# A hybrid diffusion step: modulation rows as four column tiles of 128 in place of two of 256

## What is computed

```python
def modulation(cvec, w_mod, b_mod):              # w_mod: 1024 x 6144
    m = (jax.nn.silu(cvec) @ w_mod + b_mod)[..., None, :]
    return jnp.split(m, 6, axis=-1)              # sh1, sc1, gt1, sh2, sc2, gt2

def ada_norm(x, g, shift, scale):
    return rmsnorm(x, g) * (1.0 + scale) + shift

for l in range(DEPTH):                           # DEPTH = 2
    h = ada_norm(x, g_pre_mix[l], sh1, sc1)
    y = mixer(h, ...)
    x = x + gt1 * rmsnorm(y, g_post_mix[l])
    h = ada_norm(x, g_pre_ffn[l], sh2, sc2)
    y = hier_moe(h, ...)
    x = x + gt2 * rmsnorm(y, g_post_ffn[l])
```

## The kernel before

| blocks | place |
|---|---|
| 0, 1 | start of the neighbourhood attention, after the context scores and after the first unit's scores |
| 2, 3 | start of the latent attention, in the same two positions |
| 4 | inside the loop of the latent attention, at unit 16 |
| 5 | after the latent attention, before the gates and branches are merged |
| 6 to 11 | the tail, among transposes, router logits (L1300 copies them), counting and listing of the experts' tokens |

## Time and profile before

### The profile page before, as it was taken

How to read it: one execution, slowest core, us unless ns; L and a number is a source line. 1 busy time by engine, 2 the same in 40 slices (tenths; PEclk the granted TensorE clock), 3 DMA queues, 4 the chain that set the end, 5 groups by cost and what they waited for, 6 DMA issues and landing times.

```text
span 2179.6 us, 29979 instructions
## 1 busy us (share of the span) xinstructions
PE 1911.7 (88%) x12236; PEld 1532.5 (70%) x12236; DVE 780.6 (36%) x1418; ACT 564.7 (26%) x909; POOL 191.4 (9%) x200
## 2 busy tenths in 40 slices
PE   3799898999999796999818998989999997979992
PEld 1798555779999453878618975656899993548781
DVE  2422557652322135111062227477432222341113
ACT  1411251642211021111152104426331211201113
POOL 0102410000000000011050032100000000000104
PEclk8799999999999898999958999999999998989996
DMA  9313342211221408999682123121122214289995
GB/s 349 131 61 81 138 147 106 70 59 59 88 68 59 183 34 311 357 353 356 237 307 83 56 56 138 40 78 59 59 83 73 78 49 183 105 303 358 356 344 203
DMA packets 193262, 340.91 MB, mean 156 GB/s; under 512 B 9884, under 2 KB 113708, under 8 KB 192812
## 3 DMA queue, kind: packets, MB, share of 16 engines
q1 hardware_dynamic: 163644, 266.16, 35.4%
q10 hardware_dynamic: 21728, 44.83, 5.9%
q0 software_dynamic: 7776, 28.32, 3.7%
HBM read 309.50 MB, written 41.30 MB: 161 GB/s over the span
## 4 chain that ended last, share of the span: by engine, by line
PE 77%; DVE 10%; DMA 5%; issue 3%; ACT 3%; SPq 1%; POOL 1%; ACTq 0%; DVEq 0%; POOLq 0%
PE pair L1596 68%; PE opair L1596 5%; PE pair L1642 3%; DMA ring<-in_w_out 2%; DVE mid L1178 1%; DMA r<-mod_rows 1%; DMA ring<-in_w_up 1%; DVE r L1434 1%; ACT r L959 1%; SPq L533 1%; DVE mid L1190 1%; DMA ysT<-in_mod_aux 0%; DVE mid L1070 0%; DVE mid L1219 0%; DVE mid L1307 0%
## 5 line engine op out<-in xcount | busy, mean ns | idle before, releaser
L1596 PEld LDWEIGHTS pair<-r,ring 128*128 128x128 f32 x2176 | 252.5, 195 | 22.0 <-issue 19.4
L1596 PE MATMUL pair<-r,ring 128*128 128x128 f32 x2176 | 253.0, 278 | 6.0 <-DMA ring<-in_w_up 6.0
L1596 PE MATMUL pair<-ring,r 128*128 128x512 f32 x456 | 207.8, 611 | 34.1 <-DMA ring<-in_w_out 31.1
L1596 PE MATMUL pair<-hT_r,mid_r 128*128 128x320 f32 x768 | 237.3, 309 | 0.0
L1596 PE MATMUL pair<-r_r,ring_r 128*128 128x320 f32 x832 | 211.8, 309 | 2.2 <-DVE ring_r L1051 2.2
L1642 PE MATMUL pair<-cst,mid 128*128 128x128 f32 (+1 forms) x668 | 107.3, 300 | 112.2 <-DVE mid L1070 81.6
L1642 PEld LDWEIGHTS pair<-cst,mid 128*128 128x128 f32 (+1 forms) x668 | 81.9, 152 | 156.9 <-DVE mid L1070 85.8
L1596 PE MATMUL pair<-ysT_r,mid_r 128*128 128x256 f32 (+1 forms) x768 | 172.0, 315 | 16.3 <-issue 16.3
L1596 PEld LDWEIGHTS pair<-ring,r 128*128 128x128 f32 x456 | 86.7, 195 | 140.2 <-issue 132.2
L1596 PE MATMUL pair<-mid_r 128*128 128x320 f32 x576 | 178.9, 311 | 1.6 <-issue 1.6
L1596 PE MATMUL pair<-r_r,mid_r 128*128 128x256 f32 (+2 forms) x576 | 180.0, 313 | 0.0
(11 more groups left out here) (248 smaller groups left out, 2949.7 us busy)
## 6 DMA issues: line engine op xcount, KB each, us to landing
ring<-in_w_mod SPq DMA_DIRECT2D x27, 2048.0 KB, 9.6
ring<-in_w_gate SPq DMA_DIRECT2D x34, 1024.0 KB, 7.3
ring<-in_w_up SPq DMA_DIRECT2D x34, 1024.0 KB, 12.5
ring<-in_w_down SPq DMA_DIRECT2D x34, 1024.0 KB, 11.1
ring<-in_w_in SPq DMA_DIRECT2D x24, 1024.0 KB, 7.1
expert_out<-r ACTq DMA_DIRECT2D x34, 512.0 KB, 7.5
ring<-in_w_in SPq DMA_DIRECT2D x8, 2048.0 KB, 13.8
ring<-in_w_branch SPq DMA_DIRECT2D x12, 1024.0 KB, 5.1
```

What stands on the lines that cost most here:

```text
L1596: return nc.tensor.matmul(out, lhsT, rhs, start=first, stop=last, skip_group_check=True)
```

## The change

The two constants become 4 and 128: a block is four column tiles of 128 columns, with results at output partitions 0, 32, 64 and 96. All helpers take their loops from `MT` and their widths from `MW`.

```diff
 MOD = 6 * D
 NMOD = MOD // 512
-MT, MW = 2, 256
+MT, MW = 4, 128
 EPS = 1e-6
```

## The result

The changed kernel takes 2206.54 us, the median of 4 runs (2204.61 to 2209.29); the kernel before, run beside it, 2178.25 (4 runs, 2177.26 to 2179.66). The ratio is 1.0130, 95% interval 1.0115 to 1.0145: **+28.3 us**. Measured again later, with 4 and 15 runs, it was 2206.19 against 2179.61, ratio 1.0119 (1.0104 to 1.0135). The forecast was +13.9 us, with 2199 as the upper end. The direction was right, the size half.

The account below looks back on a forecast made before the run. TensorE held 77% of the chain of waits, but its saving counted only where waited for. Terms of +6.8 us a layer, 13.6 for two, plus prologue 0.3 gave +13.9 on 2177.66: 2191.6 us, range 2180 to 2199.

Parts of the forecast that it names:

- TensorE's block: Each modulation block on TensorE: four tiles side by side take 1.9 us, saving 1.7 us a block.
- that rival: Modulation blocks on TensorE: four tiles don't share the array, product stays at 3.6 us; +19.5 us, 2197; chance 0.13.
- VectorE: Reading and scaling each block's tiles: 8 operations instead of 4, 2.4 us, +0.67 us a block.
- The overlap rival: Block rows on VectorE: short operations overlap, rows stay 1.7 us; +2.8 us in all, 2180.5; chance 0.17.
- Prologue: Four blocks before the layers: stores issued 3.5 us later find free engines; +0.3 us, bounds 0 and +3.5.
- C: Block 4, inside the latent loop: VectorE's maximum waits for TensorE, so the shorter product counts; −1.7 us a layer.
- D: Block 5, before the merge: product hidden, VectorE's rows and the stores lengthen the chain; +1.3 us a layer.
- A: Start of the neighbourhood attention: VectorE waits for later loads, then works longer; +3.3 us a layer.
- B: Start of the latent attention: later loads and longer VectorE rows, the product's saving hidden; +1.4 us a layer.
- E: The tail: block 7 −1.1, VectorE's rows +1.34, SyncE's queue before the first expert's weights +2.3; +2.5 us a layer.
- the clock falls: TensorE at half clock in first units of both attentions; +4 us a layer, 2199.6; chance 0.12.

Follow-up runs that it names:

- b_dve: The kernel before with each VectorE operation of a modulation block cut in two column halves, 8 a block; 2181.69 us, +2.4.
- a_byrow: The changed kernel with one DMA per conditioning row instead of per tile, 2 loads and 2 stores a block; 2187.73 us, +9.5 against the kernel before.
- b_pe4: The kernel before with four TensorE tiles, rows kept in two-tile layout, 6 VectorE operations, 2 loads and 2 stores a block; 2179.95 us, ratio 1.0004.
- a_twice: The changed kernel with the layers' modulation products computed twice; 2207.28 us, +27.9 against the kernel before.
- b_sp_dve: The kernel before with SyncE's loads and stores and VectorE's operations doubled, TensorE's blocks left as they were; 2204.96 us, +25.6.
- the fill: 64 unread TensorE records added behind each of blocks 0, 1, 2, 3 and 5 of a layer; on the kernel before 2180.49 us, +2.1.
- a_fill: The changed kernel with 64 unread TensorE records added behind each of blocks 0, 1, 2, 3 and 5 of a layer; 2205.32 us, +27.0 against the kernel before.
- the tail's fill: The changed kernel with 64 unread TensorE records added behind blocks 6, 8 and 9 only; 2206.52 us, against 2206.19 without.
- b_pe4_twice: The four-tile kernel with two-tile rows (`b_pe4`) with every block's products computed twice; 2186.70 us, +8.4 against the kernel before.

## Why the prediction was half right

**TensorE's block: right.** 64 records in 1.93 us at full clock, forecast 1.9. The four tiles share the array; that rival is out.

**VectorE: right.** 2.4 us a block, forecast 2.4. The overlap rival named its own test, starts under 0.25 us apart; they are 0.29 to 0.31 apart. `b_dve` shows that the rival's mechanism exists (0.21), but only between operations on the same partitions. VectorE's part grew from 1.73 to 2.44 us a block while TensorE's shrank from 3.62 to 1.93. The Trainium skill, TensorEngine Tiling (Array Packing), Performance Considerations, says that packing speeds up TensorE but not the evacuation of PSUM, and that this should be vectorized over tiles. The trace agrees that it was not sped up. For the vectorizing no run stands alone: between `a_byrow` (8 operations, 2187.7) and `b_pe4` (6 operations and other stores, 2180.0) lie 7.8 us.

**Prologue: right.** The four stores are issued at 39.41 and the last has landed at 41.63, forecast 41; VectorE's first normalisation starts 0.88 us later, forecast 0.3. Kernels with the old prologue start it up to 1.0 later than the trace before, so this is not told from the forecast, nor from nothing.

**C and D: right.** C is 13.32 us for 15.01 between the two maxima named at `a_twice`, in both layers, so -1.7 (the table of the result, from another start, has -2.0); D is +1.25. The forecast was -1.7 and +1.3.

**A: too small.** Forecast +3.3, measured +3.86 by the chain above, in the second layer +3.9. I had counted the four loads as +1.7; they are +2.16, because the third does not follow the second at once (issues at 255.97, 256.84, 258.11 and 258.96).

**B and the first term of E: the step that failed, and by the cause that I had as a rival.** The forecast put TensorE's work behind the lengthened waits at no extra time. It runs at half clock.

For B the forecast was +1.4. Measured were about +3.2 and +3.4 (in the first layer later by 2.6 before it and by 5.8 behind it; in the second 16.3 and 19.7). The SyncE and VectorE terms came as forecast: the copy L1164 at B is 1.3 and 1.4 us later than the place's first L1155. Behind it the half clock adds 1.7, of which 0.3 is won back. The other 0.6 lies between A and B, where six transposes take 1.54 us for 0.87.

The rival "the clock falls" priced this at 4 us a layer for A and B together; I gave it 0.12 and put nothing of it into the sum, and it left the tail out. Its objection, that the stretches are short and covered by the waits, holds at A (`a_byrow`) and failed at B and in the tail. What the clock costs is shown on `b_sp_dve`: the fill alone takes 7.2 us back. Half right the rival was in its cause, too: I wrote "a 1.9 us block and a longer wait". `b_sp_dve`, with blocks of 3.6 us, shows that the wait suffices, and `b_pe4` that the shorter block does.

**E: the largest miss, +5.7 and +4.4 us for +2.5.** Along the chain of waits, first and second layer:

| term | forecast | measured |
|---|---|---|
| block 7, to the last logits' copy | -1.1 | +1.6, +1.3 |
| VectorE's rows, to block 9's first store (853.54 before, 861.93) | +1.34 | +1.4, +1.4 |
| SyncE's queue, to the first expert's weights (858.53 before, 869.16) | +2.3 | +2.2, +2.2 |
| their landing | 0 | +0.4, -0.7 |

VectorE's and SyncE's terms are right. The first is wrong by 2.7 and 2.4 us: the block is 1.56 us shorter, but the logits and transposes in front of it take 2.4 us more at half clock, a cost that the sum did not have; the rows behind it take the forecast's 0.7 more. In `a_byrow` TensorE's wait there is the same 3.80 us and the stretch up to the last logits comes out 1.8 us shorter in one layer and 0.4 longer in the other, so the same wait does not always cost the same.

**What is left of the miss.** The traces show +23.1 us, 9.2 more than forecast. The half-clock work just named, 1.4 at B, 0.6 between A and B and 2.4 in the tail, is 4.4 us a layer, 8.8 in all. This is an estimate from rows of the changed kernel; no run took it out of this kernel.

**SyncE's share.** The forecast's own terms for it (A 2.3, B 0.7, D 0.6, E 2.3 a layer) are 11.8 us, and alone it costs 12.6. Within the change it is worth 17 to 19 (`a_byrow`), with the half-clock work that its waits bring. The parts don't add up, and the forecast added them.

**The scale.** I subtracted the 3.8 us by which the profiled execution lay above the median. A later set of 18 runs of the kernel before has its median at 2178.3, so some 0.6 of the miss is that; the changed kernel's profiled run lay 1.9 below its own median.

**Open.** How much of the changed kernel's 28 us a higher clock would give back. The fill takes 7.2 us off `b_sp_dve` and 3.8 off `b_pe4`, but 1 (not told from 0) off the changed kernel, and in its tail nothing. In the profiled run of `a_fill` the chain at A, from the first L1030 to the copy L1164, is 11.16 us for 11.30: there the loads set the time, and the fill changes nothing. At B it helped in one layer of two. No fill was tried that is fitted to the changed kernel's longer waits. Nor was it tried what makes a store cost more than its issue time, or why the expert's weights took 2 us longer to land behind the tail's fill.

## What to carry to other kernels

Count what a finer tiling does to everything behind the product: here each column tile has its own VectorE operations and its own DMAs, and the kernel became 28 us slower, although the shorter blocks by themselves were worth some 6 (`b_pe4_twice` less `b_pe4`). Keep the layout behind the product (`b_pe4`) and cut only the product. When two additions both lengthen a wait of TensorE, don't add them: look whether TensorE's work behind that wait was granted the full clock, and what it costs at the half one. A shorter product can lengthen such a wait by itself: TensorE is done sooner and has to wait longer for the other engines.

## What was unexpected

- Two small VectorE operations (2x128) on the same partitions start 0.21 us apart; on other partitions, 0.28 to 0.31.
- A DMA with a stride of 32 partitions took no longer as a load on SyncE (1.41 us for two, 1.47 before), but longer as a store (1.13 us for two, 0.58 before).
- Idle time of TensorE filled with 64 unread records at five places a layer made two kernels faster by 3.8 and 7.2 us and left the changed kernel as it was; on the kernel before it came out at +2.1 us, not told from nothing.
